# A hybrid decoder layer on one core: the order of norms, splits and first units, and the state of the recurrence

## The reference

```python
hn  = rmsnorm(x, w_pre_mix);  z = hn @ w_in
# 8 recurrent heads, dk=32, dv=64: S_t = diag(a_t) S_{t-1} + k_t^T v_t, o_t = q_t S_t
# 8 window heads: keys of the last 128 tokens, a distance penalty, a softmax with a sink
mix = concat(o_recurrent, o_window) @ w_out
h   = x + rmsnorm(mix, w_post_mix)
f   = rmsnorm(h, w_pre_ffn)
f   = (silu(f @ w_gate) * (f @ w_up)) @ w_down
h   = h + rmsnorm(f, w_post_ffn)
h   = h + sigmoid(h @ w_ple_gate) * (p @ w_ple_proj)
```

## Time and profile before

| what | us |
|---|---|
| median of 3 runs | 2829.82 |
| lowest and highest | 2828.7, 2829.92 |
| the profiled execution | 2830.93 |
| its span, first to last instruction | 2828.8 |
| mean granted share of PE's clock in it | 0.985 |

### The profile page before, as it was taken

How to read it: one execution, slowest core, us unless ns; L and a number is a source line. 1 busy time by engine, 2 the same in 40 slices (tenths; PEclk the granted TensorE clock), 3 DMA queues, 4 the chain that set the end, 5 groups by cost and what they waited for, 6 DMA issues and landing times.

```text
span 2828.8 us, 38154 instructions
## 1 busy us (share of the span) xinstructions
PE 2714.7 (96%) x15072; PEld 2263.8 (80%) x15072; DVE 1209.9 (43%) x2110; ACT 851.0 (30%) x1680; POOL 238.5 (8%) x416
## 2 busy tenths in 40 slices
PE   6999999999999979999999999999999989999987
PEld 4777777877777759978777777877777979999987
DVE  5455552555555473134433556344234461111143
ACT  4344532443334343122222243332222331000021
POOL 0033000111100000111110002121210000000000
PEclk9999999999999999999999999999999999999998
DMA  7865577777776676745544576444445665444453
GB/s 252 299 205 181 202 289 238 263 253 249 243 246 237 252 283 199 235 159 181 180 153 175 201 247 204 161 161 160 150 155 182 233 216 188 164 164 164 164 183 123
DMA packets 215777, 579.40 MB, mean 205 GB/s; under 512 B 28320, under 2 KB 66080, under 8 KB 215200
## 3 DMA queue, kind: packets, MB, share of 16 engines
q1 hardware_dynamic: 214960, 574.87, 58.7%
q0 software_dynamic: 640, 2.10, 0.2%
HBM read 430.41 MB, written 147.65 MB: 204 GB/s over the span
## 4 chain that ended last, share of the span: by engine, by line
PE 85%; DVE 7%; DMA 3%; ACT 2%; issue 2%; SPq 1%; POOL 0%; DVEq 0%; ACTq 0%; POOLq 0%
PE ps L1862 75%; PE ps L1935 2%; DMA wld<-wl 1%; PE ps L1955 1%; PE ps L2013 1%; PE ps L2048 1%; DVE wl L1467 1%; DVE bl L1562 1%; PE ps L2032 1%; DVE ssq L1519 1%; PE ps L2037 1%; DMA wl<-wld 1%; PE ps L1871 1%; PE ps L2002 1%; DVE mixF L1543 1%
## 5 line engine op out<-in xcount | busy, mean ns | idle before, releaser
L1862 PE MATMUL ps<-bh,wh 128*128 128x512 f32 (+1 forms) x2352 | 774.3, 363 | 9.6 <-DVE bl L1562 5.3
L1862 PE MATMUL ps<-bl,wh 128*128 128x512 f32 (+1 forms) x2352 | 757.9, 356 | 0.0
L1862 PE MATMUL ps<-bh,wl 128*128 128x512 f32 (+1 forms) x2352 | 757.8, 356 | 0.0
L1862 PEld LDWEIGHTS ps<-bh,wh 128*128 128x128 f32 x2352 | 418.0, 189 | 84.6 <-issue 12.0
L1862 PEld LDWEIGHTS ps<-bh,wl 128*128 128x128 f32 x2352 | 418.3, 189 | 63.1
L1862 PEld LDWEIGHTS ps<-bl,wh 128*128 128x128 f32 x2352 | 418.6, 189 | 58.6 <-issue 1.7
L1862 PE MATMUL ps<-gh,wh 128*128 128x512 f32 (+1 forms) x880 | 291.9, 364 | 15.7 <-DVE mixF L1491 8.6
L1862 PE MATMUL ps<-gl,wh 128*128 128x512 f32 (+1 forms) x880 | 285.6, 357 | 0.0
L1862 PE MATMUL ps<-gh,wl 128*128 128x512 f32 (+1 forms) x880 | 285.3, 357 | 0.0
L1862 PE MATMUL ps<-dh,wh 128*128 128x512 f32 (+1 forms) x768 | 263.9, 374 | 17.5 <-DVE dl L1562 9.6
L1862 PE MATMUL ps<-dl,wh 128*128 128x512 f32 (+1 forms) x768 | 255.1, 363 | 0.0
(11 more groups left out here) (191 smaller groups left out, 2860.1 us busy)
## 6 DMA issues: line engine op xcount, KB each, us to landing
wh<-whd SPq DMA_DIRECT2D x306, 512.0 KB, 3.6
wl<-wld SPq DMA_DIRECT2D x306, 512.0 KB, 4.5
w_raw<-in_w SPq DMA_DIRECT2D x102, 512.0 KB, 4.6
whd<-wh SPq DMA_DIRECT2D x102, 512.0 KB, 5.5
wld<-wl SPq DMA_DIRECT2D x102, 512.0 KB, 6.2
zt<-zd SPq DMA_DIRECT2D x16, 1024.0 KB, 7.8
zd<-zst SPq DMA_DIRECT2D x56, 256.0 KB, 5.0
res_m<-in_x SPq DMA_DIRECT2D x24, 256.0 KB, 6.1
```

What stands on the lines that cost most here:

```text
L1862: last = MM(out, ww[SLOT[n]][:, w_], xx[:, kk, r_], start=(j == 0 and x == 0), stop=(j == len(ks) - 1 and x == 2))
```

## The change

- The norms M1, M2, M3 square the blocks of the mix while `out` still runs, at its parts 12 to 14 and the first part behind it (`squares_of_mix`); their mean is at part 0 of `ple` in place of part 6, their `nm` starts at part 4 in place of 8 or 9. X3's squares are at 8 in place of 11, its mean at 11 in place of 13; F2 and F3 (`embedding_norm`) have squares at 6 and 8 in place of 10 and 12, mean at 11 in place of 13. In `z`0 the gate steps start at part 4 in place of 1, and X1's mean is at 11 in place of 10.
- `PAIRED`: the first two units of `z`0, and the first two `ple` units of chunk 3, are worked block by block together. The split of the second weight unit stands ahead of the first norm's root. In `ple`3 P3's `nm` and `sp` hang at part 4 in place of 2.
- `BY_PART`: units of `z`0 and `z`1, and each phase's first unit where it has one group, run first all eight high x high products, then high x low, then low x high, and wait for each kind only when they come to it.
- `o_split`: the mix's early splits hang two blocks at a time at the last four parts of `ffn`, in place of all at one part.
- State: `Sc` and `Sdc` keep the state by head, 2 x 64 columns. PE makes the update in 32-column tiles, eight small products with 64 columns each; DVE multiplies the old state with the decay and adds the update (two operations of 128 x 64 a state); POOL spreads `Sc` into `S` with one operation, on prompt tiles alone. The state is stored with one DMA in place of four; for the samples it is loaded both ways.

The core of the diff:

```diff
+PAIRED = [FIRST[("z", 0)], FIRST[("ple", 3)] + 2]
+BY_PART = {_n for _n in range(NU) if len(UNITS[_n].groups) == 1
+           and (any(BOUNDS[_ph][0] <= _n < BOUNDS[_ph][1] for _ph in (("z", 0), ("z", 1))) or _n in FIRST.values())
+           and _n not in PAIRED and _n - 1 not in PAIRED}
...
 def embedding_norm(kind, c, name):
-    beside(kind, c, 10, "sq", name, [0, 1, 2, 3])
-    beside(kind, c, 12, "sq", name, [4, 5, 6, 7])
-    norm_steps(kind, c, name, None, 13, 16, sp=True)
+    beside(kind, c, 6, "sq", name, [0, 1, 2, 3])
+    beside(kind, c, 8, "sq", name, [4, 5, 6, 7])
+    norm_steps(kind, c, name, None, 11, 14, sp=True)
+def squares_of_mix(c):
+    for i, ks in ((12, [0, 1, 2, 3]), (13, [4, 5]), (14, [6]), (16, [7])):
+        beside("out", c, i, "sq", f"M{c}", ks)
...
-    if early:
-        beside("ffn", c - 1, 2 * len(FFN) - 2, "sp", f"O{c}", OUT_K[0:early])
+    for i in range(0, early, 2):
+        beside("ffn", c - 1, 2 * len(FFN) - 4 + i // 2, "sp", f"O{c}", OUT_K[i:i + 2])
...
-    gate_steps("z", 0, 1, 0)
-    norm_steps("z", 0, "X1", 7, 10, 13, sp=True)
+    gate_steps("z", 0, 4, 0)
+    norm_steps("z", 0, "X1", 7, 11, 14, sp=True)
...
+    squares_of_mix(1)
...
-    norm_steps("ple", 0, "M1", 4, 6, 9)
-    norm_steps("ple", 0, "X3", 11, 13, 16)
+    norm_steps("ple", 0, "M1", None, 0, 4)
+    norm_steps("ple", 0, "X3", 8, 11, 14)
...
+    squares_of_mix(2)
...
-    norm_steps("ple", 1, "M2", 4, 6, 8)
+    norm_steps("ple", 1, "M2", None, 0, 4)
...
+    squares_of_mix(3)
...
-    norm_steps("ple", 2, "M3", 4, 6, 8)
+    norm_steps("ple", 2, "M3", None, 0, 4)
...
-            beside("ple", 3, 2, s, "P3", [2 * i, 2 * i + 1])
+            beside("ple", 3, 4, s, "P3", [2 * i, 2 * i + 1])
...
             def load_state(s):
...
+                sp.dma_start(Sdc[:, :, :, :].rearrange("p b q v -> p (b q v)"),
+                             A["state"][:, s * DB * 2 * DV:(s + 1) * DB * 2 * DV]).then_inc(sv_in, 16)
...
             def state(t):
                 gp.wait_ge(t_o.sem, t_o.at(t, 1))
-                for n, (b, r_) in enumerate(spans(t)):
-                    gp.wait_ge(v_um.sem, v_um.at(t, b + 1))
-                    s_ = S[:, :, :] if t < NT else Sd[:, b, :, :]
-                    TT(s_, s_, eg[:, :, r_.stop - 1:r_.stop].broadcast_to([P, 2, 4 * DV]), ALU.mult
-                       ).then_inc(p_s.sem, 1)
-                    gp.wait_ge(p_s.sem, p_s.at(t, 2 * n + 1))
-                    TT(s_, s_, (um1 if b else um)[:, :, :], ALU.add).then_inc(p_s.sem, 1)
+                gp.wait_ge(v_um.sem, v_um.at(t, 2))
+                TT(S[:, :, :].rearrange("p q (h v) -> p q h v", h=4),
+                   Sc[:, :, :].rearrange("p q (h v) -> p q h v", h=1).broadcast_to([P, 2, 4, DV]),
+                   head_mask[:, :].rearrange("p (a h v) -> p a h v", a=1, v=1).broadcast_to([P, 2, 4, DV]), ALU.mult
+                   ).then_inc(p_s.sem, 1)
...
             split(0)
+            split(1)
             root("X0")
...
-                    if n + 1 < NU and p == PART0[n] and RAW[n + 1]:
+                    if 0 < n < NU - 1 and p == PART0[n] and RAW[n + 1]:
                         split(n + 1)
...
             def update(t):
-                for b, _ in spans(t):
+                dve.wait_ge(a_eg.sem, a_eg.at(t, 1))
+                for b, r_ in spans(t):
                     dve.wait_ge(t_u.sem, t_u.at(t, b + 1))
...
-                    V.tensor_tensor((um1 if b else um)[:, :, :], ps[:, 2 + b, :].rearrange("p (q n) -> p q n", q=2),
-                                    block_mask[:, :].rearrange("p (a n) -> p a n", a=1)
-                                    .broadcast_to([P, 2, 4 * DV]), ALU.mult).then_inc(v_um.sem, 1)
...
+                    for q in range(2):
+                        s_ = Sc[:, q, :] if t < NT else Sdc[:, b, q, :]
+                        V.scalar_tensor_tensor(s_, s_, eg[:, q, r_.stop - 1:r_.stop], ps[:, 2 + b, q * DV:(q + 1) * DV],
+                                               ALU.mult, ALU.add).then_inc(v_um.sem, 1)
...
+            def by_part(n, part, first):
+                u, g = UNITS[n], G0[n]
+                ks = u.groups[0][1]
+                todo = [(x, k, blk) for x in range(3) for k, blk in ks]
+                if part == 0 and g >= 2:
+                    pe.wait_ge(*evicted(g - 2))
+                for y in range(24 * part // PARTS[n], 24 * (part + 1) // PARTS[n]):
+                    x, k, blk = todo[y]
+                    if y == 16 and RAW[n]:
+                        pe.wait_ge(w_lod, RAW_NO[n] + 1)
+                    if first and x == 0:
+                        pe.wait_ge(a_hi, split_val(operand_name(u), k))
+                    elif first and x == 1:
+                        pe.wait_ge(a_lo, split_val(operand_name(u), k))
+                    mm = products(n, g, k, blk, (x,), y == 0, y == 23)
+                    if y == 23:
+                        mm.then_inc(gd, 1)
+            def pair(n, part):
...
+                total = PARTS[n] + PARTS[n + 1]
+                for b in range(8 * part // total, 8 * (part + 1) // total):
+                    k, blk = UNITS[n].groups[0][1][b]
+                    pe.wait_ge(a_lo, split_val(operand_name(UNITS[n]), k))
+                    for m in (n, n + 1):
+                        mm = products(m, G0[m], k, blk, (0, 1, 2), b == 0, b == 7)
+                        if b == 7:
+                            mm.then_inc(gd, 1)
...
                 if part == 0:
-                    if RAW[n]:
+                    if not RAW[n]:
+                        pe.wait_ge(w_parts[SLOT[n]], 32 * CACHED_IN[n])
+                    elif n in BY_PART:
+                        pe.wait_ge(w_hi, RAW_NO[n] + 1)
+                    else:
                         pe.wait_ge(w_lod, RAW_NO[n] + 1)
...
                     for q in range(2):
-                        lhs = ktok[:, q * P:(q + 1) * P] if t < NT else ktok2[0:w, b, q * P:(q + 1) * P]
-                        last = MM(ps[:, 2 + b, q * 4 * DV:(q + 1) * 4 * DV], lhs,
-                                  vtok[0:w, q * 4 * DV:(q + 1) * 4 * DV], start=True, stop=True)
+                        for hh in range(4):
+                            at, k_ = q * P + DK * hh, 4 * q + hh
+                            lhs = ktok[:, at:at + DK] if t < NT else ktok2[0:w, b, at:at + DK]
+                            last = MM(ps[DK * hh:DK * hh + DK, 2 + b, q * DV:(q + 1) * DV], lhs,
+                                      vtok[0:w, k_ * DV:(k_ + 1) * DV], start=True, stop=True)
```

More of the change, by code:

```diff
@@ L415, in build @@
         Sd = sb("Sd", [P, DB, 2, 4 * DV])
+        Sc = sb("Sc", [P, 2, DV])
+        Sdc = sb("Sdc", [P, DB, 2, DV])
         kw = [sb(f"kw{s}", [P, 2, P]) for s in range(2)]
@@ L868, in tile @@
                     if s == 15:
[L869 to L872, removed]
+                        sp.wait_ge(v_um.sem, v_um.at(t, 2))
+                        sp.dma_start(O["state_p"], Sc[:, :, :]).then_inc(last_out, 16)
                 if t >= NT:
@@ L878, in tile @@
                     if s == 9:
[L879 to L885, removed]
+                        sp.wait_ge(v_um.sem, v_um.at(t, 2 * DB))
+                        sp.dma_start(O["state"][:, j * DB * 2 * DV:(j + 1) * DB * 2 * DV],
+                                     Sdc[:, :, :, :].rearrange("p b q v -> p (b q v)")).then_inc(s_out, 16)
                         if j + 1 < NS:
-                            sp.wait_ge(s_out, 64 * (j + 1))
+                            sp.wait_ge(s_out, 16 * (j + 1))
+                            sp.wait_ge(t_o.sem, t_o.at(t, 1))
                             sp.wait_ge(t_pv.sem, t_pv.at(t, 1))
@@ L1068, in tile @@
                     diff(t, 6)
-                elif s == (8 if sample else 15):
+                elif s == 15:
                     state(t)
@@ L1277, in ends @@
                 act.wait_ge(p_gend.sem, p_gend.at(t, 1 if t < NT else DB))
-                if p_s.at(t, 0) > 0:
-                    act.wait_ge(p_s.sem, p_s.at(t, 0))
+                if v_um.at(t, 0) > 0:
+                    act.wait_ge(v_um.sem, v_um.at(t, 0))
+                if p_qe.at(t, 0) > 0:
+                    act.wait_ge(p_qe.sem, p_qe.at(t, 0))
                 A_(eg[:, :, 0:w], zs(t, ZG, ZG + 2), ACT.Exp, scale=1 / GATE_NORM).then_inc(a_eg.sem, 1)
@@ L1832, in operand, with operand_name, products @@
                 return split_at({"z": "X", "out": "O", "g": "F", "u": "F", "ple": "P"}[u.kind] + str(u.c))
+            def operand_name(u):
+                return {"z": "X", "out": "O", "g": "F", "ple": "P"}[u.kind] + str(u.c)
+            def products(n, g, k, blk, kinds, first, last_):
+                u = UNITS[n]
+                xh, xl = operand(u)
+                for x in kinds:
+                    ww, xx = ((wh, xh), (wh, xl), (wl, xh))[x]
+                    for hh, r_ in halves(u.c):
+                        out = ps[:, 4 + 2 * (g % 2) + hh, 0:HW] if wide(u.c) else ps[:, 5 + 2 * (g % 2), :]
```

(19 more changed lines are left out.)

39 lines of the change are left out of this document (22 added, 17 removed).

## The result

The changed kernel takes 2765.9 us (median; 2762.6 to 2770.0), the kernel before 2829.7. The ratio is 0.9777 (95% interval 0.9765 to 0.9789): 63 us less; 70 were forecast. The spans of the two profiled executions, 2828.8 and 2764.1, are 64.7 apart.

A forecast was written before the change was run, and what follows sets the result against it. TensorE (PE), busy 2714.7 of 2828.8 us, was taken as the bound, so its waits, half clock and cheaper work count. Terms sum to -70.5 from 2830.93, 2760.4 (median 2759.3), stated as 2760 us; range 2746 to 2796.

The forecast's parts named there:

- Norm waits, -29.0: PE's waits at the norms' mean matmuls, 44.7 us, go except the start's 15.2 and 0.5 at M1: -29.0.
- Half clock, -11.9: Six stretches at 1.2 GHz behind waits to be removed, 23.7 us together, go with those waits: -11.9 us.
- Splits of the mix, -7.5: End of `ffn`, three places: low parts spread two blocks a part no longer delay the `dn` eviction: -7.5 us.
- Start and kinds in `z` 0, -0.6 and -1.8: `z` 0: pairing the first units saves a net 0.6 us; by kinds, the wait of 1.79 at 62.87 goes, -1.8.
- Kinds at phase starts, -1: First units of `out` 0 and `z` 3 worked by kinds: -1 us for both, between -3 and +3.
- Last phase, -10.3: `ple` 3: splits at part 4 and the pair let PE work where it stood: -10.3 us, bounds -7 and -12.
- Update, -8.4: State update in 32-column tiles: 0.4 us saved on twelve prompt tiles, 0.9 on four sample tiles, nothing on the first four.
- the price of 0.3 a switch: State update: if each tiling switch in and out took 0.3 us on sixteen tiles, 9.6 us, its saving would be gone.
- `ple` 0 and `z` 3, -15.9: The stretch `ple` 0 with `z` 3: the forecast's terms for it come to -15.9 us.
- rival 4: `ple`: weight loads queue behind M's blocks on SP, residual loads make DVE late in three phases; slower, 2840 us; chance 0.04.
- signs of being right: No later mean wait over 1 us, clock 1.0 through `ple` 0 to 2, `ple` 3 starting earlier, update under 0.7 us.
- signs of being wrong: Waits at `ple` part 0 for block 7's squares, for weight loads at parts 5 to 9, over 3 us behind the first pair; update over 1 us.

The follow-up runs named there:

- wide update: State update, state, its load and stores put back as before (four products of 128 x 256 a state) in the changed kernel: 2773.0 us, ratio 0.9808.
- norms only: The kernel before with only the norms M1 to M3, X3, F2 and F3 hung as in the changed kernel: 2796.7 us, ratio 0.9896.
- later levels: The changed kernel with PE's third and fourth level of the first four tiles one step later, behind six more dense products: 2759.9 us, ratio 0.9755.

## Why the prediction held, and where it was off

The total came out at 63 of the 70 us forecast. By parts, the norm waits, the splits and the last phase came as forecast, `z` 0, `ffn` 0 and `ffn` 2 gave more, and two stretches gave back 12 us by mechanisms that the forecast had at nothing.

*Norm waits, -29.0.* 44.7 became 16.0: -28.7, with 0.69 in place of 0.5 at M1. X3 has one part more between its last sum and its mean, not two as the forecast says; its wait of 9.82 went all the same. But not every wait that went was won; see `ple` 0 below.

*Half clock, -11.9.* The six stretches went, as said. The step that failed is the silent one that none would be added: `z` 1 has +5.1, `ple` 0 +2.5 and `z` 3 +1.7, where in the kernel before none followed a wait of 2.90. Two that the term did not name went as well (1.7 in `ffn` 0, 1.9 in `ple` 3). Over all, PE work at half clock fell from 50.0 to 35.7 us, which is worth 7.2.

*Splits of the mix, -7.5.* -8.0 in the waits; undone, +9. Two blocks a part did fit.

*Start and kinds in `z` 0, -0.6 and -1.8.* The stretch gave -8.1 with X1, 2.3 more than the terms. A wait of 0.93 for the high part of unit 2 came behind the pair, where 1.2 was forecast. Without the order by kinds the stretch is 3.9 us longer by the profile (23.91 to 146.31, against 23.30 to 141.79), so by this profile the term for kinds was too small.

*Kinds at phase starts, -1.* `out` 0's wait fell from 4.66 to 2.24 and `z` 3's from 2.90 to 1.35, but the first unit then takes longer, as the forecast warned. From the first product of the unit ahead of the wait to the 24th product behind it, the kernel after is 1.8 us faster at `out` 0 than the run without kinds (308.98 to 325.80, against 309.87 to 328.48) and no faster at `z` 3 (1023.25 to 1036.72, against 1027.07 to 1040.55). By the times of the whole kernel without kinds, +2 remains unsettled.

*Last phase, -10.3.* -10.3. The first unit began at 2703.03, against 2702.6 forecast (2757 less the 54.4 saved before `ple` 3), the unit behind the pair at 2720.64 against 2719.3 (2772.5 + 1.2 - 54.4); its wait of 1.32 was forecast as 1.2. The 1.3 kept for a slow clock in the pair wasn't needed (no half clock stands there), but the pair ended 1.2 later than forecast. That the two cancel is luck.

*Update, -8.4.* Twelve and four tiles gave 11.2. In `z` 1, "nothing on the first four tiles" was wrong by 5.1: the wait behind takes up the saved half microsecond, as said, but a longer wait isn't free when PE's clock falls behind it. Undone as a whole the update costs 9 by the times, near the 8.4, but only because the two errors go opposite ways. The Trainium skill (TensorEngine Tiling (Array Packing), Key Properties) says that a change of tiling mode drains TensorE. What can be seen of it here is small: from the last dense product to the first record of the update it is 0.33 us now (613.12 to 613.45) and was 0.23 (166.98 to 167.21). Whether this 0.1 is the drain isn't shown; with all of it in, a prompt tile still gains 0.49, so the price of 0.3 a switch that the forecast tried does not hold. Nor did the tiles run one behind another; the forecast's +16.6 for that is 16.4 by its own factors.

*`ple` 0 and `z` 3, -15.9.* Of the 8.2 us that are missing here, the forecast's terms for M1 explain most. Its wait of 2.31 fell to 0.69 and the half clock behind it went. But from the first product of `ple` 0 to the first of its third `ple` unit it is 29.7 us now (960.72 to 990.45) and was 29.3 (972.11 to 1001.44): nothing was won up to there. What the norm's wait and the slow clock had covered is the late store. In the kernel before, ACT, the landing times of the stores of low parts in `ple` 0, and PE:

```profile
998.19 1.06 ACT L1101 ACTIVATE wh<-w_raw 128x1024 fp32r<-128x1024 f32 x1 [1.14 <-DMA wld<-wl]
```
```profile
DMA to landing us min/median/max: 6.1/7.4/11.0
```
```profile
1001.44 0.40 PE L1862 MATMUL ps<-dh,wh 128*128 128x512 f32 x1
```

The store took 11.0 us there too (11.3 now; 6.2 is the page's median), ACT waited for it, and PE came late enough not to wait. Behind that place the kernel after loses more by its new half clock and by the next late weight: at the fifth unit it is 4.0 us behind (45.6 against 41.6 from the first product of `ple` 0). X3's mean then gives 13.2, and `z` 3 takes 1.5 back.

So rival 4 had the place (weights behind M's blocks in `ple`) and the wrong size and link. M1's stores, which the earlier norm brings into this stretch, don't make the store slow: it took 11.0 us in the kernel before, where they start only at 1010.60, and the wait stayed with the stores moved. X3's input, which comes at the same part in both kernels, does matter: with it loaded earlier the store lands in 8.4 us and the wait is 1.64. SP also issues that store sooner then (11.9 us behind the first product of `ple` 0 in place of 16.0, as eight loads no longer stand ahead of it); how much is the fuller DMA engines and how much the queue is not separated. In sum 3.7 us of waits for split weights (6.1 against 1.55 + 0.85), 2.5 of clock there and 1.7 in `z` 3 are 7.9 of the 8.2, not 24 a phase; as `z` 3's own wait came out 1.0 better than its term, about 1 us has no account.

Of the signs of being right, the granted clock of 1.0 through `ple` 0 to 2 failed in `ple` 0 (0.91 from 960 to 1000). Of the signs of being wrong, waits for weights did come at parts 6 and 8 of `ple` 0 (1.09 and 3.92), for split weights and not for loaded ones.

## What to carry to other kernels

A product made faster ahead of a wait for another engine wins nothing and lengthens the pause; look then at the granted clock behind that pause, and put independent products into it. Before a wait is counted as won, look for what was only just in time behind it, here a store that takes 11 us; and sum the bytes in such a stretch, since moving 2.4 MB of loads out of it brought the store to 8.4. Before undoing or adding one part of a bundle, ask which other part needs its timing: with the old norms the order by kinds cost 3.9 and 4.4 us at two phase starts, where high parts come late.

## What the runs showed of the hardware

Pauses of about 1.9 us in `z` 1 (four a run) were followed by half clock at two or three of the four places in all seven profiles that have them; pauses of 1.4 to 1.5 us at none, none and one of four (before, wide update, norms only); pauses of 0.4 never in two profiles. Between the kernel with the wide update and the kernel after, each of the three pauses with half clock behind it made `z` 1 longer by 1.5 us (4.6 in all, where half of the PE work in them makes 5.1), and the one without it by nothing. The length alone doesn't settle it: in the run with later levels a wait of 3.21 us at 143.37 was followed by no such stretch, while 2.75 at 141.79 in the kernel after was.
